# Gathers of 128 rows instead of 96 in a mixture-of-experts layer, and an index copy moved from VectorE to ScalarE

## The chip, the core and the metric

The kernel runs on one core of a Trainium2 chip. The core has five engines that run side by side: TensorE (PE; its weight loads are shown apart as PEld), VectorE (DVE), ScalarE (ACT), GpSimd (POOL) and SyncE (SP). They meet only through semaphores. Data moves between HBM and on-chip memory (SBUF) through 16 DMA engines, which the queues of SP and of POOL share. The metric is the device time of one execution in microseconds (us); less is better. Before the change it is 1160.18 us, the median of 3 runs (1159.56 to 1162.26).

## The reference

One decoder layer for 512 tokens of width 1024: two attention branches, and then a mixture of experts (MoE). Only the second part matters here:

```python
scores = jax.nn.sigmoid(h @ w_router)                      # 64 experts
_, top_idx = lax.top_k(scores + router_bias, 8)            # 8 experts for a token
top_w = take(scores, top_idx) / sum(...) * 2.5
...
hg = xb @ w_gate_e[e];  hu = xb @ w_up_e[e]                # 1024 -> 256, for each expert
hmid = silu(hg) * hu * gate
routed += hmid @ w_down_e[e]                               # 256 -> 1024
...
x = x1 + routed + swiglu(h, w_gate_s, w_up_s, w_down_s)    # a shared expert for all tokens
```

512 tokens with 8 experts each are 4096 pairs of token and expert, 64 to an expert in the mean. All weights and activations are float32.

## The kernel before

The first part of the program computes attention and the routing. The second, from about 500 us on, is a pipeline over 68 items: 4 tiles of tokens through the shared expert (`SH = 4`), then 64 experts. The change lies in the pipeline of the experts.

An expert has `SLOTS = 96` slots. A matmul against a one-hot matrix (`find_slots`) finds the token of each slot, and `read_idx` (line 1258, VectorE) writes the token indices to `idxg`, one to a partition. A slot without a token gets an index of 1024 or more (`NO_TOKEN`), which lies above the bounds check (511), and the DMA skips its row. Which slot stands on which partition is set by a table made on the host, line 1822, with `DMA_ENGINES = 16`:

```python
c[:, P:P + SLOTS] = np.arange(SLOTS).reshape(SLOTS // DMA_ENGINES, DMA_ENGINES).T.reshape(-1)[None]
```

Partitions 0 to 5 so hold slots 0, 16, 32, 48, 64 and 80, partitions 6 to 11 slots 1, 17, 33 and so on.

For expert k the work goes through the engines as follows.

- **SP** loads the expert's three weights (1 MB each) into one of four slots (`load_w`, line 470). A load waits until the expert four places earlier has been split.
- **POOL** gathers the expert's token rows (4 KB each) from `hn_dram` into `xg` (line 566), up to five experts ahead, and later adds the expert's output rows to `out` in HBM (the scatter, line 572). The loop `pair` issues scatter k and then gather k + 5. A scatter waits until the one before has landed. Ahead of each transfer stands a tiny operation, `turn` (line 562), that keeps their order.
- **ScalarE** (`step`) rounds weights to their high parts (`gu_hi_k`, line 863; `split_wd`, line 814), applies SiLU, copies the turned tokens, and writes the output rows to one of two buffers `y` (line 831), for which the scatter of two experts earlier must have landed.
- **VectorE** (`expert`) subtracts to get the low parts of the weights (lines 1290 and 1300), multiplies by the gate, and makes the indices and one-hot matrices of later experts.
- **PE** multiplies with three products of high and low parts for each matmul (lines 1669 and 1683), turns the gathered rows (line 1697), and finds slots.

Each engine's program is a fixed list in this order; a semaphore wait holds back all that stands behind it. `idxg` is overwritten for expert k + 4 before the scatter of k may have been issued, so a second copy, `idxs`, is made for the scatter (line 1397, VectorE), and the semaphore `idx_kept` counts these copies.

Of the kernel before, what the change touches and what calls it, by code (L numbers as in the profile page):

```python
# [41 lines left out]
SLOTS = 96  # L42
DMA_ENGINES = 16
WARM_UP = 56
NO_TOKEN = 1024
# [4 lines left out]
def layer(nc, x, g_mix, w_in, q_norm_a, k_norm_a, q_norm_b, k_norm_b, rel_bias, b_forget, w_gate, b_gate,  # L50
# [98 lines left out]
    with ctx:  # L149
# [25 lines left out]
        idxg = [sb(f"idxg{i}", [P, 1], u32) for i in range(4)]  # L175
# [150 lines left out]
        def after(eng, s, n):  # L326

            if not isinstance(n, int) or n > 0:
                eng.wait_ge(s, n)  # L329
# [199 lines left out]
        def _(pool):  # L529
            nc.gpsimd.memset(minus_half[:], -0.5).then_inc(pool_set, 1)  # L530
            pool.wait_ge(pool_set, 1)

            def root(dst, src, n, width):

# [18 lines left out]
                pool.wait_ge(tr_ready[b], uses[b])  # L553
            for i in range(4):
                nc.gpsimd.memset(xg[i], 0.0).then_inc(pool_set, 1)
            pool.wait_ge(pool_set, 5)
            last_row = pool.to_reg(N - 1)

            def take_turn(before):
# [3 lines left out]

            def gather(slot, before, done):
                take_turn(before)
                pool.indirect_dma_start(out=xg[slot][0:SLOTS, :], out_offset=None, in_=hn_dram,  # L566
                                        in_offset=bass.IndirectOffsetOnAxis(idxg[slot][0:SLOTS, 0:1], 0),
                                        bounds_check=last_row, oob_is_err=False).then_inc(done, 16)

            def scatter(slot, idx, before, done):  # L570
# [48 lines left out]
        def _(act):  # L619
# [246 lines left out]
            def xT_hi_k(k):  # L866
# [4 lines left out]
                for c in range(2):  # L871
                    nc.scalar.activation(xT_hi[:, c * HALF:(c + 1) * HALF, :], turned_rows(c), ACT.Copy).then_inc(xT_hi_ready, 1)

            def step(it, n, slot, more=True):
                k = it - SH
                if more:
                    for c in range(CHUNKS - 1):
                        gu_hi_k(k + 1, (slot + 1) % 4, c)
# [17 lines left out]
            for it in range(SH):  # L896
# [9 lines left out]
                if it == SH - 2:  # L906

                    act.wait_ge(hn_ready, NT)
                    act.wait_ge(onehot_ready, 1)
                    act.wait_ge(logits_psum, 1)  # L910
                    for c in range(CHUNKS - 1):
                        gu_hi_k(0, 0, c)
            for c in range(CHUNKS - 1):
                gu_hi_k(1, 1, c)
            silu_i(SH, 0, SLOTS)
# [32 lines left out]
        def _(dve):  # L948
# [432 lines left out]
            def expert(k, u, ix=True, oh=True, xt=True):  # L1381
# [11 lines left out]
                    low_wd(u, 0, last_hi, last_lo).then_inc(wd_ready, 1)  # L1393
                if isinstance(k, int) and k == 0:
                    y_shared(SH - 1)
                after(dve, scattered, 16 * (k - 3))
                nc.vector.tensor_copy(idxs[u][0:SLOTS, :], idxg[u][0:SLOTS, :]).then_inc(idx_kept, 1)
                low_midT_i(SH + k, u % 2, SLOTS)
                if ix:
                    dve.wait_ge(mid_ready, SH + k + 1)  # L1400
# [457 lines left out]
```

## Time and profile before

| | |
|---|---|
| median of 3 runs | 1160.18 us (1159.56 to 1162.26) |
| profiled execution, device time | 1161.51 us |
| its span in the profile | 1159.5 us |
| PE busy | 1112.1 us (96%) |
| DVE busy | 875.7 us (76%) |
| ACT busy | 719.9 us (62%) |
| POOL busy | 363.3 us (31%) |
| DMA | 284.64 MB, mean 245 GB/s, 65606 packets |
| clock granted to PE, mean | 0.986 of full |

The profile is of one execution. Its span runs from the first to the last instruction; the device time has 2.0 us more around it. An engine's busy share is a mean over the whole program, and stages differ, so the rows below are mostly of stretches. "L863" is line 863 of the kernel; the releaser behind an arrow is what ended the idle time. The DMA share is the mean over 16 engines of the time that their packets took; packets overlap a little, so it can exceed 1. PE's busy time is modelled and PE at 100% need not be at its peak.

### The profile page before, as it was taken

What the parts mean: (1) busy time and instruction counts of PE and PEld (TensorE: products, weight loads), DVE (VectorE), ACT (ScalarE), POOL (GpSimd) and SP (SyncE); (2) the same over time, 40 slices, a digit from 0 to 9 for tenths busy, and PEclk for the clock granted to TensorE, in tenths of its full rate; (3) what the DMA queues carried; (4) which work ended last, traced back from release to release, by engine and by line L of the source; (5) the groups of instructions that cost most, each with busy time, mean ns of one, the idle gap of its engine ahead of it and who ended that gap; (6) DMA issues with size and microseconds to landing.
All of it is one profiled execution on the core that took longest, in us unless ns stands there. A gap on an engine that the chain in (4) does not pass through costs nothing.

```text
span 1159.5 us, 18735 instructions
## 1 busy us (share of the span) xinstructions
PE 1112.1 (96%) x5682; PEld 826.2 (71%) x5682; DVE 875.7 (76%) x1445; ACT 719.9 (62%) x1218; POOL 363.3 (31%) x293
## 2 busy tenths in 40 slices
PE   7999999999999999999999999999999999989994
PEld 5889978777775575567777777777676767766762
DVE  6443476578753534589999999989898989989982
ACT  5434455453435121268888888878787878877882
POOL 0221021000000001136333344344345344568842
PEclk7999999999999999999999999999999999999998
DMA  5333221412422275459999999999999999999952
GB/s 188 123 96 119 78 74 37 155 65 78 123 85 80 67 324 209 159 216 384 368 365 365 370 372 367 367 364 371 366 367 367 355 359 365 371 361 357 365 184 34
DMA packets 65606, 284.64 MB, mean 245 GB/s; under 512 B 12515, under 2 KB 15083, under 8 KB 40604
## 3 DMA queue, kind: packets, MB, share of 16 engines
q1 hardware_dynamic: 51228, 250.50, 57.5%
q0 software_dynamic: 14336, 33.59, 12.2%
q8 instruction: 25, 0.41, 0.1%
q14 instruction: 17, 0.14, 0.0%
HBM read 271.40 MB, written 29.42 MB: 259 GB/s over the span
## 4 chain that ended last, share of the span: by engine, by line
DMA 47%; POOL 4%; issue 3%; POOLq 1%; ACT 0%; DVE 0%
DMA out<-arena,idxs 47%; POOL turn L562 4%; POOLq L329 0%; POOL out L572 0%; POOLq L578 0%; ACT arena L831 0%; POOL arena L566 0%; POOLq L598 0%; POOLq L582 0%; DVE w_lo L1295 0%; POOLq L583 0%
## 5 line engine op out<-in xcount | busy, mean ns | idle before, releaser
L1669 PE MATMUL bank<-gu_parts,xT_parts 128*96 128x512 f32 x1280 | 343.8, 398 | 3.1 <-DVE xT_parts L1283 2.5
L562 POOL TENSOR_TENSOR turn<-minus_half 16x1 f32<-16x1 f32 x128 | 174.1, 1360 | 341.9 <-DMA out<-arena,idxs 289.2
L1669 PEld LDWEIGHTS bank<-gu_parts,xT_parts 128*96 128x96 f32 x1280 | 202.5, 162 | 86.2 <-DVE xT_parts L1283 2.9
L1683 PE MATMUL bank<-w_lo 128*96 128x512 f32 (+1 forms) x804 | 200.3, 397 | 0.9 <-DVE w_lo L1295 0.9
L1683 PEld LDWEIGHTS bank<-w_lo 128*96 128x96 f32 (+1 forms) x804 | 128.0, 166 | 46.7 <-DVE w_lo L1295 1.1
L1500 PE MATMUL bank<-w_hi,hT_hi 128*128 128x512 f32 (+1 forms) x320 | 125.8, 393 | 3.1 <-DVE arena L1241 1.7
L1290 DVE TENSOR_TENSOR gu_parts<-arena_x,gu_parts 128x1024 fp32r<-128x1024 f32 x96 | 116.7, 1215 | 12.5 <-ACT gu_parts L863 12.5
L1290 DVE TENSOR_TENSOR gu_parts<-arena,gu_parts 128x1024 fp32r<-128x1024 f32 x96 | 116.6, 1215 | 11.3 <-ACT gu_parts L863 11.3
L1500 PE MATMUL bank<-w_hi,hT_lo 128*128 128x512 f32 (+1 forms) x320 | 122.7, 383 | 0.0
L1500 PE MATMUL bank<-w_lo,hT_hi 128*128 128x512 f32 (+1 forms) x320 | 122.4, 383 | 0.0
L863 ACT ACTIVATE gu_parts<-arena_x 128x1024 fp32r<-128x1024 f32 x96 | 101.4, 1056 | 27.6 <-DMA arena_x<-in_w_up_e 18.8
L863 ACT ACTIVATE gu_parts<-arena 128x1024 fp32r<-128x1024 f32 x96 | 101.4, 1056 | 24.0 <-DMA arena<-in_w_up_e 20.1
L572 POOL DMA_INDIRECT out<-arena,idxs x64 | 107.3, 1676 | 16.2 <-issue 14.2
L991 DVE TENSOR_TENSOR w_lo<-arena,w_hi 128x512 fp32r<-128x512 f32 (+1 forms) x112 | 69.1, 667 | 47.9 <-ACT w_hi L648 47.9
L831 ACT ACTIVATE arena<-bank 96x512 f32<-96x512 f32 x128 | 73.2, 591 | 31.5 <-PE bank L1683 19.9
L1669 PE MATMUL bank<-gu_more,xT_parts 128*96 128x512 f32 x256 | 90.8, 395 | 0.0
L536 POOL TENSOR_TENSOR hn_r<-hn_ms,minus_half 128x1 f32<-128x1 f32 x8 | 4.4, 555 | 254.7 <-DVE hn_ms L961 254.7
L536 POOL TENSOR_TENSOR rnorm<-mean,minus_half 128x8 f32<-128x8 f32 x20 | 32.7, 1637 | 156.5 <-DVE mean L1054 156.5
L648 ACT ACTIVATE w_hi<-arena 128x512 fp32r<-128x512 f32 (+1 forms) x112 | 61.4, 605 | 32.1 <-PE bank L1500 20.5
L1697 PEld LDWEIGHTS bank<-cst,arena 96*128 96x128 f32 x512 | 66.5, 203 | 15.2 <-DMA arena<-hn_dram,idxg 7.1
L1300 DVE TENSOR_TENSOR w_lo<-arena_x,w_lo 128x1024 fp32r<-128x1024 f32 x64 | 75.2, 1214 | 1.2 <-ACT w_lo L814 1.2
L1300 DVE TENSOR_TENSOR w_lo<-arena,w_lo 128x1024 fp32r<-128x1024 f32 x64 | 75.2, 1214 | 0.9 <-ACT w_lo L814 0.9
(194 smaller groups left out, 1934.9 us busy)
## 6 DMA issues: line engine op xcount, KB each, us to landing
arena<-in_w_gate_e SPq DMA_DIRECT2D x32, 1024.0 KB
arena<-in_w_up_e SPq DMA_DIRECT2D x32, 1024.0 KB
arena<-in_w_down_e SPq DMA_DIRECT2D x32, 1024.0 KB
arena_x<-in_w_gate_e SPq DMA_DIRECT2D x32, 1024.0 KB
arena_x<-in_w_up_e SPq DMA_DIRECT2D x32, 1024.0 KB
arena_x<-in_w_down_e SPq DMA_DIRECT2D x32, 1024.0 KB
arena<-in_w_in SPq DMA_DIRECT2D x14, 1024.0 KB, 5.4
arena<-in_w_gate SPq DMA_DIRECT2D x8, 1024.0 KB, 5.8
```

What stands on the lines that cost most here:

```text
L562: nc.gpsimd.tensor_tensor(turn[:], minus_half[0:16, 0:1], minus_half[0:16, 0:1], ALU.add).then_inc(turns, 1)
L572: pool.indirect_dma_start(out=out_rows, out_offset=bass.IndirectOffsetOnAxis(idx[0:SLOTS, 0:1], 0), in_=y[slot][0:SLOTS, :], in_offset=Non ...
L648: nc.scalar.activation(split_of(w_hi, c, j), raw_of(c, j), ACT.Copy).then_inc(split_hi, 1)
L831: return nc.scalar.activation(y[n][0:SLOTS, h * 512:(h + 1) * 512], psY[h][0:SLOTS, :], ACT.Copy)
L863: nc.scalar.activation(gu_hi[c].rearrange("p g j c -> p g (j c)"), wgu[slot][:, :, PER * c:PER * (c + 1), :].rearrange("p g j c -> p g (j ...
L991: nc.vector.tensor_tensor(split_of(w_lo, c, j), raw_of(c, j), split_of(w_hi, c, j).bitcast(f32), ALU.subtract).then_inc(split_lo, 1)
L1290: nc.vector.tensor_tensor(flat(gu_lo[c]), flat(raw_part), flat(gu_hi[c]).bitcast(f32), ALU.subtract).then_inc(gu_lo_ready, 1)
L1300: return nc.vector.tensor_tensor(low[:, :, cols], wd[slot][:, :, cols], high[:, :, cols].bitcast(f32), ALU.subtract)
L1500: last = nc.tensor.matmul(psD[n % 2][:, 0:chunk_cols(c)], left, right, start=(j == 0 and k == 0), stop=(j == ND - 1 and k == 2))
L1669: last = nc.tensor.matmul(out_, a[:, PER * c + j, :], b[c][:, :, j, :], start=(c == 0 and j == 0 and i == 0), stop=(c == CHUNKS - 1 and j ...
L1683: last = nc.tensor.matmul(psY[h][0:rows, :], midT[n][a][:, j, 0:rows], w[b][:, j, h * 512:(h + 1) * 512], start=(j == 0 and k == 0), stop= ...
L1697: last = nc.tensor.transpose(psT[j // HALF][:, c:c + SLOTS], xg[slot][0:SLOTS, j::ND], ident[0:SLOTS, 0:SLOTS])
```

## The change

A gather now has 128 rows. Its index list is the whole of `idxg`, whose last 32 entries are set once, at the start, to `NO_TOKEN` and never again, so the last 32 rows are always skipped. The slot table of line 1822, the scatter (96 rows) and the number of transfers stay. The copy of `idxg` to `idxs` goes from VectorE, where it stood behind the expert's last gate and up split, to ScalarE, at the head of each `step`. The diff:

```diff
@@ POOL @@
             nc.gpsimd.memset(minus_half[:], -0.5).then_inc(pool_set, 1)
             pool.wait_ge(pool_set, 1)
+            for i in range(4):
+                nc.gpsimd.memset(idxg[i][SLOTS:, :], NO_TOKEN).then_inc(pool_set, 1)
+                pool.wait_ge(pool_set, i + 2)
...
-            pool.wait_ge(pool_set, 5)
+            pool.wait_ge(pool_set, 9)
...
             def gather(slot, before, done):
                 take_turn(before)
-                pool.indirect_dma_start(out=xg[slot][0:SLOTS, :], out_offset=None, in_=hn_dram,
-                                        in_offset=bass.IndirectOffsetOnAxis(idxg[slot][0:SLOTS, 0:1], 0),
+                pool.indirect_dma_start(out=xg[slot], out_offset=None, in_=hn_dram,
+                                        in_offset=bass.IndirectOffsetOnAxis(idxg[slot][:, 0:1], 0),
                                         bounds_check=last_row, oob_is_err=False).then_inc(done, 16)
@@ ScalarE @@
+            def keep_idx(k, u):
+                act.wait_ge(idx_ready, k + 1)
+                after(act, scattered, 16 * (k - 3))
+                nc.scalar.activation(idxs[u][0:SLOTS, :], idxg[u][0:SLOTS, :], ACT.Copy).then_inc(idx_kept, 1)
+
             def step(it, n, slot, more=True):
                 k = it - SH
+                keep_idx(k, slot)
                 if more:
...
+            keep_idx(0, 0)
             for c in range(CHUNKS - 1):
                 gu_hi_k(1, 1, c)
@@ VectorE @@
-                after(dve, scattered, 16 * (k - 3))
-                nc.vector.tensor_copy(idxs[u][0:SLOTS, :], idxg[u][0:SLOTS, :]).then_inc(idx_kept, 1)
                 low_midT_i(SH + k, u % 2, SLOTS)
```

POOL's list in the loop over experts, before and after. A row is an instruction with its line, what it writes and reads, its shape, and the semaphores it waits for:

```order
L566 DMA arena<-hn_dram,idxg 96x1024
L582 REGISTER_ALU
L329 REGISTER_ALU [waits idx_kept,y_ready]
L329 ISA [waits scattered]
L562 TENSOR_TENSOR turn<-minus_half 16x1 [waits turns]
L572 DMA out<-arena,idxs 512x1024
```

```order
L569 DMA arena<-hn_dram,idxg 128x1024
L585 REGISTER_ALU
L329 REGISTER_ALU [waits idx_kept,y_ready]
L329 ISA [waits scattered]
L565 TENSOR_TENSOR turn<-minus_half 16x1 [waits turns]
L575 DMA out<-arena,idxs 512x1024
```

Only the gather's rows have changed, 96 to 128; order and waits are the same (512x1024 is the whole of `out`; the scatter's index list still has 96 entries).

ScalarE's list around the end of one step and the start of the next, in the loop, before and after:

```order
L814 ACTIVATE w_lo<-arena 128x2x512 [waits y_psum] x2
L924 REGISTER_ALU
L924 COMPARE_AND_BRANCH
L863 ACTIVATE gu_parts<-arena_x 128x1024 [waits gu_part,w_slot1_u,w_slot1_g]
L863 ACTIVATE gu_more<-arena_x 128x1024 [waits gu_part,w_slot1_u,w_slot1_g]
```

```order
L817 ACTIVATE w_lo<-arena 128x2x512 [waits y_psum] x2
L934 REGISTER_ALU
L934 COMPARE_AND_BRANCH
L880 ACTIVATE idxs<-idxg 96x1 [waits scattered,idx_ready]
L866 ACTIVATE gu_parts<-arena_x 128x1024 [waits gu_part,w_slot1_u,w_slot1_g]
L866 ACTIVATE gu_more<-arena_x 128x1024 [waits gu_part,w_slot1_u,w_slot1_g]
```

The index copy, with its two waits, stands ahead of the first weight split of each step. On VectorE it is gone, and nothing else has moved there.

## Rows read from the trace of the kernel before

**Rows 1.** The page's 40 slices: PE and DMA in tenths busy, GB/s.

```profile
PE   7999999999999999999999999999999999989994
...
DMA  5333221412422275459999999999999999999952
GB/s 188 123 96 119 78 74 37 155 65 78 123 85 80 67 324 209 159 216 384 368 365 365 370 372 367 367 364 371 366 367 367 355 359 365 371 361 357 365 184 34
```

**Rows 2.** Busy time by stretch; then PEclk, DMA share, GB/s.

```profile
core 0: us, PE busy (x) PEld busy (x) DVE busy (x) ACT busy (x) POOL busy (x), PEclk, DMA share, GB/s
450.00:500.00 50.00, 46.25 (x173) 24.79 (x172) 26.67 (x75) 9.90 (x17) 7.87 (x10) 1.00 0.57 220
525.00:575.00 50.00, 50.00 (x263) 37.40 (x263) 49.16 (x73) 42.81 (x63) 24.79 (x18) 1.00 1.02 378
575.00:775.00 200.00, 199.50 (x1034) 148.12 (x1033) 193.18 (x292) 171.04 (x248) 81.95 (x84) 1.00 1.03 367
775.00:1000.00 225.00, 219.17 (x1098) 160.32 (x1097) 204.25 (x308) 178.50 (x264) 99.68 (x87) 0.99 1.02 365
1000.00:1120.00 120.00, 112.77 (x571) 81.87 (x570) 107.30 (x155) 93.92 (x138) 86.91 (x46) 1.00 0.98 346
1120.00:1160.00 40.00, 23.21 (x108) 16.40 (x106) 17.45 (x25) 17.48 (x27) 12.04 (x10) 0.86 0.25 36
```

**Rows 3.** Waits from 550 to 775 us, total, times, longest.

```profile
ACT gu_parts L863 <- DMA arena<-in_w_up_e: 2.9, 2, 1.8
```

**Rows 4.** Waits from 775 to 1120 us.

```profile
ACT gu_parts L863 <- DMA arena_x<-in_w_up_e: 18.6, 10, 3.3
ACT gu_parts L863 <- DMA arena<-in_w_up_e: 17.3, 8, 3.3
ACT arena L831 <- DMA out<-arena,idxs: 11.1, 10, 4.5
```

**Rows 5.** POOL in order of time (start, duration), 680 to 694 us.

```profile
681.79 1.45 POOL L572 DMA_INDIRECT out<-arena,idxs  x1 [0.16 <-issue]
...
690.02 1.23 POOL L562 TENSOR_TENSOR turn<-minus_half 16x1 f32<-16x1 f32 x1 [4.78 <-DMA out<-arena,idxs]
691.40 1.45 POOL L572 DMA_INDIRECT out<-arena,idxs  x1 [0.16 <-issue]
```

**Rows 6.** Two scatters on POOL, from 790 us.

```profile
790.42 1.45 POOL L572 DMA_INDIRECT out<-arena,idxs  x1 [0.16 <-issue]
...
800.33 1.45 POOL L572 DMA_INDIRECT out<-arena,idxs  x1 [0.16 <-issue]
```

**Rows 7.** The page's DMA queues: packets, bytes, share of 16 engines.

```profile
q1 hardware_dynamic: 51228, 250.50, 57.5%
q0 software_dynamic: 14336, 33.59, 12.2%
```

**Rows 8.** Issues of expert weights: ns min/median/max, first and last start.

```profile
L470 SPq DMA_DIRECT2D arena<-in_w_down_e x32: 328/333/515, 408.0 to 1105.5; - x32
```

**Rows 9.** The page's chain that ended last.

```profile
DMA 47%; POOL 4%; issue 3%; POOLq 1%; ACT 0%; DVE 0%
```

**Rows 10.** Line 572, the scatter, issue to landing.

```profile
DMA to landing us min/median/max: 4.6/8.8/11.6
```

**Rows 11.** POOL in order of time, 1038 to 1062 us.

```profile
1038.88 1.00 POOL L566 DMA_INDIRECT arena<-hn_dram,idxg  x1 [0.15 <-issue]
...
1041.35 1.45 POOL L572 DMA_INDIRECT out<-arena,idxs  x1 [0.16 <-issue]
...
1051.51 1.45 POOL L572 DMA_INDIRECT out<-arena,idxs  x1 [0.16 <-issue]
```

**Rows 12.** Line 1397, VectorE's index copy, ns min/median/max.

```profile
L1397 DVE COPY idxs<-idxg x64: 138/143/147, 511.5 to 1139.8; 96x1 uint32<-96x1 uint32 x64
```

**Rows 13.** ScalarE's smallest copy, by form.

```profile
L721 ACT ACTIVATE frow<-bank 128x8 f32<-128x8 f32 x4 | 0.7, 171 | 4.4 <-PE bank L1500 4.4
```

## The prediction, made before the changed kernel was run

> **What bounds the kernel now.** I read the slices of the page first. From slice 19 on (about 525 us) PE reads 9 and the DMA line is also 9, at 355 to 384 GB/s [rows 1]. So two resources look full at once, and only a view by stage can part them. The windows do: from 525 to 1000 us the 16 DMA engines show a share of 1.02 to 1.03 (packets overlap, so a full engine reads a little over 1), from 1000 to 1120 us 0.98, and 0.25 after the last weights [rows 2]. Before, at 450 to 500 us, it was 0.57. PE is busy at full clock for 199.5 of 200 us up to 775 us, and then loses 5.8 of 225 us and 7.2 of 120 us [rows 2].
>
> Third come the waits. Up to 775 us ScalarE waits for expert weights (line 863, the first to touch them) for only 2.9 us in all, after that for 18.6 + 17.3 = 35.9 us [rows 3, 4]. That is a prefetch running out: four weight slots give a lead, PE takes an expert every 9.6 us (scatters issued at 681.79 and 691.40) [rows 5], the DMA engines take longer, and at about 775 us the lead is gone. From there an expert takes some 10 us [rows 6].
>
> What the DMA engines need can be worked out from the queues [rows 7]. The weight queue was busy 57.5% of 16 engines: 0.575 x 16 x 1159.5 = 10,667 us for 250.50 MB, or 42.6 us per MB. An expert's 3.146 MB are then 134 us, 8.4 us on each engine. The gather and scatter queue took 12.2%, 2,263 us; over 64 experts that is 35.4 us, 2.2 us on each engine. Together 10.6 us, or 10.4 at a share of 1.02: the pace seen after 775 us, and above PE's 9.6. Since the average engine has no idle time from 525 us to the last weights, the fullest has none either, and a load has landed only when all of its engines are done. The end is therefore that of the fullest DMA engine, plus a tail that doesn't change: the last w_down load is issued at 1105.5 us [rows 8], the engines are empty soon after 1120 us, and the span ends at 1159.5.
>
> The chain of waits names something else, the scatters: 47% of the span, one after the other [rows 9]. A scatter lands 8.8 us after its issue [rows 10], and the next waits for it. But what the scatters hold up is only the buffer y, and line 831 waits for that 11.1 us in all, 10 times after 775 us, against 35.9 us for weights [rows 4]. I take this chain as a second bound lying just beneath the first.
>
> **The change, part by part.** The gather. Queue 0 had 14,336 packets [rows 7]: 128 transfers of 96 rows and 16 completions are 128 x 112 = 14,336, so a skipped row is still a packet, a tiny one. Its 33.59 MB are 8,192 rows of 4,096 B, 64 x 64 gathered and as many scattered. With 32 more rows to a gather there are 64 x 32 = 2,048 more empty packets and not a byte more.
>
> What changes is who does the work. The kernel's own slot table (line 1822) puts slot s into row 6 x (s mod 16) + s div 16: six rows in a row for each of 16 DMA engines, with consecutive slots on different engines. This deals any number of tokens evenly, provided that an engine gets six consecutive rows. With 128 rows an engine gets eight, and the table is not changed. Dealt eight in a row, the 96 live rows fall on engines 0 to 11, and engines 12 to 15 gather nothing.
>
> The rows can be counted, since routing the reference's own inputs tells each expert's tokens (44 to 91, 4,096 in all). In the kernel before, the fullest engine gathers 286 rows and scatters 286, the emptiest 226 and 226. After, with eight in a row, the fullest gathers 414. The first five gathers go out ahead of all scatters, while the engines still have idle time (share 0.57 at 450 to 500 us) [rows 2]; without them it is 266 rows before and 384 after, 118 more.
>
> The Trainium skill has another deal for 128 partitions ("DMA: Bandwidth & Descriptors", the descriptor swizzle): engine 0 takes rows 0 to 3 and 32 to 35, and so on, so that engines 8 to 15 have four live rows each and engines 0 to 7 eight. By it the fullest engine gathers 376 rows from expert 5 on, 110 more, and scatters 4 fewer: 110 x 0.174 - 4 x 0.378 = 17.6 us. Nothing in this trace shows a 128-row gather; either deal has engines with eight live rows, and that is what counts.
>
> The price of a gathered row, 4,096 B: at the weight queue's 42.6 us per MB it is 0.174 us. The mean of queue 0 is 2,263 / 8,192 = 0.276 us [rows 7], over gathers and scatters. A scatter adds to what is in HBM and has to read as well, so the gather is the cheaper of the two: 0.174 is the lower end, 0.276 the upper, and I take 0.174, as a plain transfer (a scattered row is then 2 x 0.276 - 0.174 = 0.378). Sum: 118 x 0.174 = 20.5 us. As the deal isn't shown, and one with fewer live rows on the fullest engine would give less, I take 19 us. The bounds are 0 (an even deal) and 118 x 0.276 = 32.6 us.
>
> Nothing hides this: the fullest engine has no idle time, and the prefetch lead is spent already; it would only be spent sooner. Before, that engine lay 30 rows above the mean of 256 both ways, 30 x 0.552 = 16.6 us; the change more than doubles this.
>
> POOL issues a gather in 1.00 us [rows 11]; 128 rows instead of 96 may cost up to 1.33 us. Behind it stands only the next scatter, and POOL is idle 4.78 us before it, for a landing [rows 5], so nothing is lost. After 1000 us that cover is gone at times (gather at 1038.88, the next scatter 2.47 us later) [rows 11]: at most 0.33 x 12 = 4 us, if scatters set the pace there. With weights coming later still they don't, and I add nothing. The four memsets of index tails stand at the program's start, ahead of POOL's first wait for VectorE: nothing. A row of SP isn't moved, and no transfer is added.
>
> The index copy. DVE loses 64 copies of 143 ns [rows 12], 9.2 us. ScalarE gains 64; the nearest row is a 128x8 copy of 171 ns [rows 13], 10.9 us in all. Its waits stop nothing: the indices were needed by the gather long before, and the count of scatters that it wants (16(k-3)) is the one that the previous step's y copy already waited for. Behind it on ScalarE stands the first weight split of line 863, which itself waits for weights when these are late; in the stage where PE sets the pace ScalarE is busy 171 of 200 us [rows 2]. If that cover failed it would cost up to 10.9 us. DVE is busy 193 of 200 us there, and could give back up to 9.2 us if it set the pace, but a faster compute stage only runs down the lead sooner. Both zero.
>
> Sum: profiled run 1161.5 us (span 1159.5 and 2.0 around it) + 19 = 1180.5; against the median of 1160.2, 1.3 us lower, 1179. I say 1180.
>
> **The rivals.** *An even deal.* The rows of a gather could go round the engines one by one, or the index list could be split by live rows. Then only 2,048 tiny packets are added: 1160 us, within 0.2%. Against it: the slot table makes sense only for consecutive rows. Chance 11%.
>
> *Scatters set the pace.* After 1000 us the share is 0.98, and the scatters follow 10.16 us apart (1041.35 and 1051.51) [rows 11]. If their chain bounds that stage, weights have slack there, and the cost is what a gather directly ahead delays a scatter: 1.33 to 2 more live rows on an engine, each with a weight packet of 8 KB in between, (0.174 + 0.349) x 1.33 to 2 = 0.7 to 1.0 us, for some 12 to 17 experts: 8 to 17 us, middle 11, so 1171 us. Chance 12%.
>
> *Wide gathers are faster.* This one ends on the other side. If a gathered row costs the mean of 0.276 us now because an engine's six rows don't suit the way it writes them, and 0.174 once they are dealt by eight, the fullest engine goes from 266 x 0.276 = 73.4 us to 384 x 0.174 = 66.8, or 376 x 0.174 = 65.4: 7 to 8 us less, 1153 us. It decides when more than 0.085 us of a row's time goes away (266 x 0.276 = 384 x 0.191). The trace has no row for a gathered packet alone; the mean holds the dear scatters, which makes this unlikely. The Trainium skill speaks for it ("SBUF — State Buffer", section "Can I just issue two DMAs to hit both halves?"): the only way to reach all 16 ports is one transfer over all 128 partitions. No row here shows ports. Chance 7%.
>
> *The upper price.* A row costs 0.276 us or more, in queueing with weight packets: 1191 us and above. Chance 5%.
>
> **How the numbers follow.** The forecast, fuller engines at 0.15 to 0.24 us a row (110 x 0.15 = 16.5 to 118 x 0.24 = 28, so 1176 to 1189), holds 65%. A range that leaves out no more than 2 in 10 has to take in the scatters' case and the upper half of the even deal: 1160 to 1190 us. What a measurement here can tell from no change is about 0.2%, 2.3 us. Faster: 7% for wide gathers and 2% from the even deal, 0.09. Same: the rest of that, 0.09. Slower: 0.82.
>
> **What would show it.** Right: queue 0 with 16,384 packets at the same 284.64 MB; in the windows GB/s from 575 to 1120 us down by about 3%, and a mean share below 1 while weights are waited for, which an even deal can't give; line 863's waits for weights above the 2.9 + 35.9 = 38.8 us of now [rows 3, 4], starting well before 775 us; an expert every 10.3 to 10.6 us instead of some 10. Scatters as the pace: line 831's waits for DMA grow beyond those for weights. Wrong: the same GB/s and share as before, or a stage between 575 and 775 us as fast as now followed by one no slower. DVE's 64 copies gone and ScalarE's 64 near 0.17 us would show the copy; if ScalarE had idle time before them on scatters, my zero there is wrong.

## The result, and the profile after

The changed kernel takes 1151.05 us in the median of 20 runs (1140.92 to 1172.72), the kernel before 1160.12 us beside it (20 runs, 1157.49 to 1173.89): ratio 0.9891, 95% interval 0.9863 to 0.992. The forecast was 1180 us, range 1160 to 1190, with 0.09 for faster. It was wrong in sign. The ratios leave out every execution that took over 1.5% longer than the fastest of its kernel: 6 of the 20 here, 14 of 31 of wide_only and its two repeats below, and 1 of 71 of the kernel before, so a median over all runs shows less gain than a ratio. The profile below is of a second set of runs of the changed kernel (after_again, 1149.74 us, 1143.07 to 1152.68, 6 runs; ratio 0.9849, 0.9797 to 0.9901). Its span is 1150.5 us against 1159.5.

The page of the changed kernel, its slices, queues and chain:

```profile
span 1150.5 us, 18761 instructions
...
PE   7999999999999999999999999999999999898995
...
DMA  5333221422422184459999999999999999998962
GB/s 183 131 97 116 83 68 44 148 73 75 128 74 92 41 335 193 184 199 395 380 378 377 378 378 376 378 382 380 380 377 378 378 376 373 332 343 288 368 207 32
...
q1 hardware_dynamic: 51228, 250.50, 56.6%
q0 software_dynamic: 16384, 33.60, 11.8%
...
DMA 41%; PE 38%; DVE 7%; POOL 5%; issue 5%; ACT 2%; POOLq 1%; SPq 0%; ACTq 0%; DVEq 0%
```

Queue 0 has the 2,048 packets more that were counted, and 33.60 MB instead of 33.59. But more packets took less time. The share of q0 is 11.8% of a span of 1150.5, that is 0.118 x 16 x 1150.5 = 2,172 us, where before it was 2,263 [rows 7]. And q1, which the change doesn't touch, took 0.566 x 16 x 1150.5 = 10,419 us for the same 250.50 MB, where before it was 10,667. Each load of weights moves faster, though nothing was done to it: this is the first sign of the cause. PE, which was not in the chain of [rows 9], now has 38% of it.

The windows of the changed kernel, to be laid beside [rows 2]:

```profile
525.00:575.00 50.00, 50.00 (x263) 37.37 (x262) 48.85 (x69) 43.16 (x69) 29.52 (x20) 1.00 1.02 383
575.00:775.00 200.00, 200.00 (x1040) 148.72 (x1039) 192.81 (x272) 173.50 (x270) 75.62 (x83) 1.00 1.02 378
775.00:1000.00 225.00, 222.56 (x1149) 164.84 (x1148) 209.49 (x297) 187.20 (x295) 102.85 (x91) 1.00 1.01 375
1000.00:1120.00 120.00, 110.87 (x535) 80.24 (x536) 102.99 (x138) 93.43 (x147) 70.44 (x46) 0.96 0.87 304
```

The share stays at 1.02 and 1.01 up to 1000 us, so the engines are as full as they were there, but what they move rises from 367 to 378 GB/s and from 365 to 375. PE, which lost 5.8 of 225 us between 775 and 1000 us, loses 2.4. The waits for weights and for the buffer y, for [rows 3, 4]; line 863 is 866 now, and line 831 is 834. From 550 to 775 us no wait of line 866 is left. From 775 to 1120 us:

```profile
ACT arena L834 <- DMA out<-arena,idxs: 17.4, 7, 6.4
...
ACT gu_parts L866 <- DMA arena_x<-in_w_up_e: 5.8, 4, 2.6
ACT gu_parts L866 <- DMA arena<-in_w_up_e: 5.0, 6, 1.2
```

Weights are waited for 10.8 us where it was 38.8, and y for 17.4 where it was 11.1. The second bound, the scatters, lay just beneath the first, as the prediction said, and came out when the first went down. Of 28 us of waits for weights that go, the span keeps 9.

Even of these 9 us only a part belongs to the pipeline. The last scatter lands at 1152.5 us before and at 1147.5 after, 5.0 us earlier. Behind it stands GpSimd's closing instruction, DRAIN, for which all engines wait, and it takes 4.4 us less. Before, then after:

```profile
L149 POOLq DRAIN  x1: 6558/6558/6558, 1152.7 to 1152.7; - x1
```

```profile
L149 POOLq DRAIN  x1: 2194/2194/2194, 1147.7 to 1147.7; - x1
```

It is 6.558 us in all three profiled versions of the layer with gathers of 96 rows (before, copy_only, narrow_plain) and 2.194 us in all seven profiles with gathers of 128. So it comes with the wide gather, but what sets it is open: no experiment was made on it, and stream and deal, which have both widths each, show 6.920 and 1.852.

The rows for [rows 12] and [rows 10], ScalarE's index copy, and the landings of the scatter (line 575), with those of the gather (line 569) behind them:

```profile
L880 ACT ACTIVATE idxs<-idxg x64: 190/193/213, 498.1 to 1128.1; 96x1 uint32<-96x1 uint32 x64
```

```profile
DMA to landing us min/median/max: 4.4/8.6/15.1
...
DMA to landing us min/median/max: 3.6/9.6/11.3
```

### The profile page after: what moved, and what is told of

Read it like the earlier page. It is cut to its first block, busy times and chain, and to the rows that moved or that the text cites. A ratio compares the mean times of both kernels' runs of the same rounds, so it can differ in the third digit from the quotient of the medians.

```text
span 1164.9 us, 18761 instructions
## 1 busy us (share of the span) xinstructions
PE 1109.7 (95%) x5682; PEld 820.0 (70%) x5682; DVE 876.3 (75%) x1381; ACT 730.0 (63%) x1282; POOL 569.0 (49%) x297
## 3 DMA queue, kind: packets, MB, share of 16 engines
q1 hardware_dynamic: 51228, 250.50, 56.4%
q0 software_dynamic: 16384, 33.60, 12.4%
## 4 chain that ended last, share of the span: by engine, by line
PE 42%; DMA 28%; POOL 13%; DVE 7%; issue 6%; ACT 3%; POOLq 0%; SPq 0%; ACTq 0%; DVEq 0%
PE bank L1508 19%; DMA out<-arena,idxs 18%; POOL turn L565 12%; DMA arena<-hn_dram,idxg 9%; PE bank L1691 5%; PE bank L1677 4%; PE bank L1457 2%; PE bank L1665 2%; PE bank L1651 2%; PE bank L1705 1%; DVE w_lo L1001 1%; PE bank L1647 1%; DVE gu_parts L1300 1%; ACT arena L739 1%; DMA arena<-in_w_out 1%
## 5 line engine op out<-in xcount | busy, mean ns | idle before, releaser
L565 POOL TENSOR_TENSOR turn<-minus_half 16x1 f32<-16x1 f32 x128 | 357.2, 2791 | 142.4 <-DMA out<-arena,idxs 81.1
L575 POOL DMA_INDIRECT out<-arena,idxs x64 | 113.8, 1778 | 20.2 <-issue 18.0
L1705 PEld LDWEIGHTS bank<-cst,arena 96*128 96x128 f32 x512 | 64.1, 203 | 44.6 <-DMA arena<-hn_dram,idxg 25.2
L875 ACT ACTIVATE xT_parts<-bank 128x384 fp32r<-128x384 f32 x128 | 56.0, 489 | 63.1 <-PE bank L1705 63.1
L1705 PE MATMUL bank<-cst,arena 96*128 96x96 f32 x512 | 69.1, 278 | 24.6 <-DMA arena<-hn_dram,idxg 24.1
L569 POOL DMA_INDIRECT arena<-hn_dram,idxg x64 | 84.6, 1322 | 10.3 <-issue 2.3
```

The source lines that it names most:

```text
L565: nc.gpsimd.tensor_tensor(turn[:], minus_half[0:16, 0:1], minus_half[0:16, 0:1], ALU.add).then_inc(turns, 1)
L569: pool.indirect_dma_start(out=xg[slot], out_offset=None, in_=hn_dram, in_offset=bass.IndirectOffsetOnAxis(idxg[slot][:, 0:1], 0), bounds_c ...
L575: pool.indirect_dma_start(out=out_rows, out_offset=bass.IndirectOffsetOnAxis(idx[0:SLOTS, 0:1], 0), in_=y[slot][0:SLOTS, :], in_offset=Non ...
L1705: last = nc.tensor.transpose(psT[j // HALF][:, c:c + SLOTS], xg[slot][0:SLOTS, j::ND], ident[0:SLOTS, 0:SLOTS])
```

## The experiments

**Which half of the change does it?** wide_only is the kernel before with the wide gather, and VectorE still copies the indices:

```diff
-pool.wait_ge(pool_set, 5)
+for i in range(4):
+    nc.gpsimd.memset(idxg[i][SLOTS:, :], NO_TOKEN).then_inc(pool_set, 1)
+...
+pool.wait_ge(pool_set, 9)
-pool.indirect_dma_start(out=xg[slot][0:SLOTS, :], ... idxg[slot][0:SLOTS, 0:1] ...)
+pool.indirect_dma_start(out=xg[slot], ... idxg[slot][:, 0:1] ...)
```

> Only the gather's part of the change: 128 rows, index tails set once; VectorE still copies the indices. Theory 1 (the 128-row gather takes load off the DMA engines: each gathered row becomes cheaper and no longer stretches weight packets): the whole gain, ratio about 0.989, some 1148 us. Theory 2 (the gain comes from taking the 0.14 us copy off VectorE, which is nearly full): no gain, 1160 us. The prediction's own mechanism (fullest engine with eight live rows) would give 1180 us, and is all but excluded by the changed kernel's 1151.

copy_only is the other half: 96 rows, and ScalarE copies.

```diff
+def keep_idx(k, u):   # ScalarE
+    act.wait_ge(idx_ready, k + 1)
+    after(act, scattered, 16 * (k - 3))
+    nc.scalar.activation(idxs[u][0:SLOTS, :], idxg[u][0:SLOTS, :], ACT.Copy).then_inc(idx_kept, 1)
-after(dve, scattered, 16 * (k - 3))
-nc.vector.tensor_copy(idxs[u][0:SLOTS, :], idxg[u][0:SLOTS, :]).then_inc(idx_kept, 1)
```

> Only the copy's part of the change: ScalarE copies the indices, gathers have 96 rows as before. Theory 1: no change, 1160 us within 2 us. Theory 2: the whole gain, some 1150 us.

after_again is the changed kernel beside both, on the same chip.

> The changed kernel once more, on the same chip as its two halves: ratio about 0.989 to the kernel before. Theory 1 expects the weight splits on ScalarE not to wait for weights, GB/s no lower than before, and a time within 3 us of the gather's part alone. Theory 2 expects it to be as fast as the copy's part alone.

Measured, against 1165.06 us of the kernel before on that chip: wide_only 1142.62 us (1139.51 to 1174.39, 7 runs), ratio 0.9793 (0.9738 to 0.9848); copy_only 1162.25 (1156.27 to 1171.6, 12 runs), ratio 1.0004 (0.9964 to 1.0043); after_again 0.9849. The gather has all of the gain, the copy none that can be measured. After_again and wide_only overlap in their intervals, so a small price of ScalarE's copy isn't excluded, and none is shown. The windows of copy_only are those of before:

```profile
575.00:775.00 200.00, 199.50 (x1035) 148.23 (x1034) 191.21 (x270) 170.94 (x268) 80.60 (x83) 1.00 1.03 367
775.00:1000.00 225.00, 220.04 (x1102) 160.50 (x1101) 204.34 (x287) 180.23 (x288) 92.74 (x88) 1.00 1.02 367
```

**How are the rows dealt, and what does one cost?** deal computes nothing of the layer: it runs 22 indirect transfers one at a time, with chosen live rows and all others skipped. In short:

```diff
+"run6": [0, 1, 2, 3, 4, 5], "run8": [0 .. 7], "step6": [0, 6, 12 .. 90], "step16": [0, 16 .. 80],
+"four_and_four": [0, 1, 2, 3, 32, 33, 34, 35], "slots64": the places of 64 tokens by the slot table
+for each of gather 96, gather 128, scatter 96: issue, wait for its landing, next
```

> No part of the layer: gathers of 96 and of 128 rows and adding scatters of 96 rows, one at a time, each waited for, with only chosen rows live (4 KB each). Of one transfer the time from issue to landing and the number of data packets that run side by side tell which rows share an engine. Deal by consecutive rows: 6 live rows in a run land one after the other in a 96-row gather (about 6 x 0.16 us) and 8 in a run in a 128-row one. Deal by four and four: a run of 8 in a 128-row gather is split over two engines (4 x 0.16 us), and rows 0 to 3 with 32 to 35 share one (8 x 0.16 us). Deal round the engines one by one: rows 0, 16, 32 ... share one, and a run of 8 lands in one packet's time. With 64 rows live in the kernel's slot order the fullest engine has 4 rows at 96; 6 to 8 by either deal at 128. The prediction needs the last.

Measured (100.02 us in all) from the packets of each transfer: the time from the first live row's start to the last one's end, and how many were under way at once.

```
gather of 96, rows 0 to 5              6 rows   1252 ns   at most 2 at once
gather of 96, rows 0, 6, 12 .. 90     16 rows    538 ns            15
gather of 128, rows 0 to 7             8 rows    969 ns             3
gather of 128, rows 0 to 5             6 rows    682 ns             2
gather of 128, rows 0-3 and 32-35      8 rows   1732 ns             2
scatter of 96, rows 0 to 5             6 rows   2434 ns             2
scatter of 96, rows 0, 6, 12 .. 90    16 rows    749 ns            16
```

GpSimd's own rows show the same: what stands in brackets is the wait for the transfer issued one row above. First the gathers of 96 with six rows in a row and with every sixth, then those of 128 with four and four, and with all 96.

```profile
12.51 1.15 POOL L62 DMA_INDIRECT xg<-in_x,idxu  x1 [10.82 <-issue]
16.20 0.99 POOL L62 DMA_INDIRECT xg<-in_x,idxu  x1 [2.55 <-DMA xg<-in_x,idxu]
19.05 0.96 POOL L62 DMA_INDIRECT xg<-in_x,idxu  x1 [1.86 <-DMA xg<-in_x,idxu]
...
52.19 0.99 POOL L62 DMA_INDIRECT xg<-in_x,idxu  x1 [2.08 <-DMA xg<-in_x,idxu]
56.20 0.99 POOL L62 DMA_INDIRECT xg<-in_x,idxu  x1 [3.02 <-DMA xg<-in_x,idxu]
60.21 0.99 POOL L62 DMA_INDIRECT xg<-in_x,idxu  x1 [3.02 <-DMA xg<-in_x,idxu]
```

At 96 an engine has six rows in a row. At 128 the eight rows 0 to 7 go to two engines, and rows 0 to 3 with 32 to 35 are all on one: four and four. The Trainium skill has the same deal for 128 partitions ("DMA: Bandwidth & Descriptors", the descriptor swizzle). The fullest engine gathers 376 rows from expert 5 on, not 384. Alone, a gathered row takes 159 ns in the median in both widths and a scattered one 328; with 0.174 and 0.378 us the prediction was 9% and 15% too high. Issuing takes GpSimd 0.96 to 0.99 us at 96 (the very first 1.15), 0.99 to 1.01 at 128. So the deal was as feared, and the prices nearly so. Something else moved.

**Does the fullest engine set the end?** narrow_plain is the kernel before with slot s in row s, so the first tokens of each expert share engines:

```diff
-np.arange(SLOTS).reshape(SLOTS // DMA_ENGINES, DMA_ENGINES).T.reshape(-1)[None]
+np.arange(SLOTS)[None]
```

> The kernel before, with 96-row gathers and scatters, but slot s on partition s. Engines still take six rows in a run (shown by the lone transfers), so engines 0 to 6 now gather and scatter 384 rows each instead of 286 at most, and the last ones nearly none. Theory 1 (the fullest DMA engine sets the end, as the prediction had it): 98 rows more, at 0.16 to 0.19 us for a gathered and 0.32 us for a scattered row, 47 to 50 us, so some 1208 us. Rival (the engines share one limit, and only their mean counts): 1160 us, no change.

Measured 1210.8 us (1209.98 to 1213.87, 4 runs) against 1160.05: ratio 1.0435 (1.0389 to 1.048). The fullest engine scatters 98 rows more, and gathers 98 more, or 88 from expert 5 on. At 0.33 and 0.19 us (as rows measure in this kernel, below) these are 49 us, and 50.8 came. The weight packets also grew here, by 8 ns in the mean (335.9 to 343.7 ns from 525 to 1125 us), which would add 11 us and isn't in that sum. So it is shown that an uneven deal costs about what its fullest engine has more, within some 10 us. The share drops below 1, as engines that are less full idle:

```profile
575.00:775.00 200.00, 187.88 (x947) 134.84 (x947) 175.86 (x265) 151.25 (x224) 152.82 (x78) 1.00 0.97 339
775.00:1000.00 225.00, 210.35 (x1014) 151.31 (x1013) 188.08 (x281) 162.76 (x243) 83.17 (x84) 0.97 0.95 333
```

even_slots goes the other way: wide_only with a slot table that is balanced for both deals, six in a row for the scatter and four and four for the gather.

```diff
-np.arange(SLOTS).reshape(SLOTS // DMA_ENGINES, DMA_ENGINES).T.reshape(-1)[None]
+np.array(SLOT_OF)[None]     # SLOT_OF = [89, 43, 27, 83, 32, 61, 80, 1, ...]
```

> 128-row gathers, VectorE copies, and a slot table that deals live rows evenly for a gather dealt four and four and a scatter dealt by six. By rows alone the fullest engine has 128 us of gather and scatter work instead of 158 (0.16 and 0.33 us a row). Theory 1a (both: foreign partitions make rows dearer at 96, and the fullest engine still sets the pace late in the 128-row version): weights no longer arrive late anywhere, an expert every 9.6 us to the end, 1138 to 1141 us, with the landings of one load's 16 engines within 3 us of each other. Theory 1b (with 128 rows the uneven deal doesn't matter): the same as the gather's part alone, 1142 us, and landings spread as there.

Measured 1141.4 us (1140.33 to 1146.85, 5 runs), ratio 0.984 (0.9801 to 0.9879).

```profile
575.00:775.00 200.00, 200.00 (x1041) 148.76 (x1041) 194.25 (x294) 173.47 (x250) 72.38 (x84) 1.00 1.02 382
775.00:1000.00 225.00, 223.16 (x1153) 165.55 (x1152) 215.24 (x323) 191.97 (x278) 93.30 (x92) 0.99 1.01 377
```

The 16 parts of one expert's last load land apart by how uneven the engines' work was up to then. Their spread, in us:

```
expert           5      20     34     44
before          2.6     9.1   18.7   20.6
after_again     2.3     7.1   13.5   18.4
even_slots      1.7     1.6    1.8    2.2
narrow_plain    5.7    16.8   22.4   21.2
```

So the unevenness is real, in the changed kernel too, and the table takes it out. Yet it is worth little. In even_slots ScalarE waits from 550 to 1120 us neither for weights nor for y, and the last packet of weights lands at 1094.9 us, where it is 1108.6 in after_again and 1111.7 in wide_again, the profile of the wide gather alone (below). But the spans of even_slots and wide_again are 1138.9 and 1140.7 us. With wide gathers the fullest engine hardly sets the end any more; what is left is PE.

**What makes every packet faster?** stream computes nothing of the layer either: 20 loads of 1 MB run back to back in each of nine phases, and in seven of them 12 indirect transfers of 64 live rows go one after the other, of which some 7 fall beside the loads.

```diff
+PHASES = [("none", 0), ("gather", 96), ("gather", 128), ("none", 0), ("scatter", 96), ("scatter", 128),
+          ("gather", 128, live rows moved up by 32), ("gather", 96), ("gather", 128)]
```

> No part of the layer: 1 MB weight loads back to back from SyncE (20 in each phase, four in flight) beside 12 indirect transfers with 64 live rows, in nine phases: none; gathers of 96; of 128; none; scatters of 96; of 128; gathers of 128 with the live rows on partitions 32 to 127; gathers of 96; of 128. Theory 1a: a weight packet (8 KB) takes 309 ns in the median in all phases, but beside 96-row gathers a fair part take 400 ns and more, and gathered rows (4 KB) 180 ns and more in the mean; beside 128-row gathers both stay near 309 and 159. The phase of 128-row gathers with live rows on 32 to 127 is as clean. Rival (it was only the phase of the two streams in the real kernel): the same packet times at 96 and 128.

Measured (702.6 us in all), in the order of the phases: the phase, how long its loads took, the mean of a weight packet of 8 KB, the share of them above 380 ns, and the mean of a live row that starts while the loads run.

```
none          50.64 us   314.8 ns   0.005     -
gather 96     59.85      339.1      0.163   204.7 ns
gather 128    57.80      317.8      0.024   165.3
none          51.10      315.7      0.005     -
scatter 96    59.73      318.5      0.022   328.3
scatter 128   61.99      321.3      0.030   348.0
gather 128^   57.39      316.3      0.022   167.8     (^ live rows 32 to 127)
gather 96     59.08      334.8      0.141   192.9
gather 128    58.14      317.9      0.025   165.1
```

This is the effect, by itself. Beside a gather of 96 rows one weight packet in six or seven is stretched from 0.31 to over 0.38 us, and the gather's own rows take 193 to 205 ns in the mean. Beside a gather of 128 rows with the same 64 live ones it is one weight packet in forty, and the rows take 165 to 168. A scatter of 96, which reads SBUF and writes HBM, stretches few weight packets either, and with 128 rows they are no shorter (321.3 against 318.5 ns). The same in the layer, 800 to 900 us (mean and 90th percentile of a weight packet, mean of a gathered and median of a scattered row, ns; gathered and scattered packets are told apart by their durations, below and above 300):

```
before          336   418   195   327
copy_only       334   404   189   327
after_again     323   324   159   327
even_slots      322   324   160   327
```

Over all of 525 to 1125 us the means are 335.9 ns before and 327.3 in after_again for a weight packet, and 192.1 and 159.7 for a gathered row.

The likely reason is where an engine writes. By the Trainium skill ("DMA: Bandwidth & Descriptors", The descriptor swizzle) each engine of a 128-partition transfer writes the partitions of one SBUF port and no other. With six rows in a row that can't hold, so at 96 an engine would write through ports at which the weight loads keep other engines busy. The port is argued, as no row shows one, and no run varied it by itself; the stretching, its near end at 128 rows and the two deals are shown.

**Wide gather again, and the even table beside it.**

> The gather's part alone once more, beside the version with evenly dealt slots: 1142 us, ratio 0.98 to 0.985. In an undisturbed execution the fullest engine's lag behind the emptiest grows over the experts (theory 1a).

Measured 1151.14 us (1140.3 to 1172.51, 12 runs), ratio 0.987 (0.9835 to 0.9904), so the median over all runs came 9 us above the 1142 expected, and the ratio just outside the range. Its profile (span 1140.7) shows 379 and 374 GB/s:

```profile
575.00:775.00 200.00, 200.00 (x1043) 148.98 (x1042) 194.25 (x293) 173.16 (x251) 71.76 (x84) 1.00 1.02 379
775.00:1000.00 225.00, 223.34 (x1151) 165.41 (x1150) 213.77 (x322) 187.53 (x275) 99.33 (x91) 1.00 1.01 374
```

even_again is even_slots, and wide_third wide_only, side by side on another chip.

> The slot table balanced for the deal of four and four, beside the same kernel with the old table (wide_third) on the same chip. If the uneven deal (fullest engine 406 gathered rows, mean 256) still costs time once the gathers are wide, this one is 2 to 6 us faster in the median, 1140 against 1144, and its range narrower. If with wide gathers PE sets the pace for nearly the whole expert stage, the two medians lie within 2 us.

> The gather of 128 rows alone, copy on VectorE, old slot table: 1141 to 1150 us, ratio to the kernel before 0.98 to 0.99. The wider part of that range means that the chain of scatters falls behind in some executions; the balanced table should not show it if the fullest engine is what starts it.

Measured: even_again 1148.15 us (1141.38 to 1150.9, 6 runs), ratio 0.9884 (0.985 to 0.9918); wide_third 1162.44 (1141.91 to 1167.5, 12 runs), with a ratio of 0.9906 (0.9863 to 0.9948). Both medians miss what was expected (1140 us for even_again, 1141 to 1150 for wide_third), and wide_third's, over all its runs, lies above the 1159.89 of the kernel before beside it. The intervals of the ratios overlap, as those of the first pair do (0.984 and 0.987). Whether the even table is worth more than the wide gather alone isn't settled; what stands is that none of its 11 runs passed 1150.9 us, where 14 of the 31 with the wide gather alone passed 1159. It beats the kernel before in both sets, and has the lowest ratio of its set each time; that it beats the changed kernel isn't shown.

**Who holds GpSimd?** The profile of even_again is 7 us longer than that of even_slots, and one difference stands out: for a while GpSimd's turn, an addition of 16x1 before each gather and scatter, takes 6 us instead of 1. held tries VectorE as the cause. It computes nothing of the layer. In short:

```diff
+for i in range(6):                       # VectorE, back to back, by phase
+    nc.vector.tensor_tensor(lo[i], a, hi, ALU.subtract)       # both in SBUF; or one in a bank; or a copy
+pool.wait_ge(runs, n + 1)                # GpSimd: after the first of the six
+nc.gpsimd.tensor_tensor(turn, minus_half, minus_half, ALU.add)
```

> No part of the layer: VectorE runs operations on 128x1024 back to back, six to a run, and GpSimd is told to do its 16x1 addition (the turn of the gathers and scatters) when the first of the six is done. Five phases of four runs: one VectorE operation alone, then nothing; six with both operands in SBUF; six of 128x512 with one operand in a PSUM bank; six copies; six with both operands in SBUF again. If VectorE's operations with two SBUF operands hold GpSimd off, the turn takes 1.1 us in the first phase and, in the second and fifth, as long as the five operations that are left, 5 x 1.21 = 6.1 us; with one operand in a bank it takes 1.1 us. If the 5.6 to 6.6 us seen in the layer come from something else (DMA, GpSimd's own descriptors), the turn takes about 1.1 us in all five.

GpSimd's rows, one for each phase in turn: VectorE does nothing more; two operands in SBUF; one in a bank; copy; two in SBUF again.

```profile
8.54 0.18 POOL L72 TENSOR_TENSOR turn<-minus_half 16x1 f32<-16x1 f32 x1 [1.40 <-DVE lo L56]
...
20.34 1.03 POOL L72 TENSOR_TENSOR turn<-minus_half 16x1 f32<-16x1 f32 x1 [6.00 <-DVE lo L56]
...
44.71 0.18 POOL L72 TENSOR_TENSOR turn<-minus_half 16x1 f32<-16x1 f32 x1 [3.63 <-DVE lo L58]
...
59.99 0.50 POOL L72 TENSOR_TENSOR turn<-minus_half 16x1 f32<-16x1 f32 x1 [3.33 <-DVE lo L60]
...
79.06 1.04 POOL L72 TENSOR_TENSOR turn<-minus_half 16x1 f32<-16x1 f32 x1 [6.00 <-DVE lo L56]
```

The turn takes 0.18 us by itself, so the 1.1 us expected for the first phase was itself such a hold. Two SBUF operands on VectorE hold it for 1.03 us, which is to the end of the operation under way (1.22 us each), and not for the four that follow: the expectation of 6.1 us failed. Half of it is shown, that VectorE's kind of operation decides; why a hold spans five operations in the layer stays open.

## Why the prediction was wrong

*The bound* was right for the kernel before. Its DMA engines read full at a share of 1.02 to 1.03, and moving rows onto the fullest engine cost 50.8 us in narrow_plain for 49 worked out. It did not stay the bound: the changed kernel's share is 0.87 from 1000 to 1120 us, and an even deal of the wide gather's rows gains little.

*The deal* was right in what counts. The fullest engine gathers 110 rows more from expert 5 on (four and four), and the spread of landings shows it still uneven.

*The price of a row* was nearly right: 0.159 us against 0.174 taken, and 0.328 against 0.378 for a scattered one. The 110 rows cost 110 x 0.159 = 17.5 us, less 4 x 0.328 = 1.3: 16.2, where the forecast had 19.

*The step that failed* is one that the prediction never wrote down as a term: that the packets which were there already keep their durations. "With 32 more rows to a gather there are 64 x 32 = 2,048 more empty packets and not a byte more" was followed by "What changes is who does the work", and by nothing on how long the work of everyone else takes. On the fullest engine, from expert 5 on (59 experts, 24 weight packets each), with the means of 525 to 1125 us:

```
more rows                  +110 x 0.159 - 4 x 0.328           +16.2 us
gathered rows, unstretched  266 x (0.1921 - 0.1597)            -8.6
weight packets              59 x 24 x (0.3359 - 0.3273)       -12.2
sum                                                            -4.6
```

The sum has the sign, and the larger term is in the weight queue, on which the change has no line. It doesn't have the size. The last packet of weights lands 15.1 us earlier in after_again (1123.7 to 1108.6 us) and 12.0 earlier in wide_again, whose weight packets are at 325.2 ns, for a sum of -7.6. The means are over all engines, and no row tells which engine a packet is on, so what the fullest one gained beyond them stays open.

A second step failed, "a tail that doesn't change". From the last packet of weights to the end of the span it is 35.8 us before, 41.9 in after_again and 29.0 in wide_again. GpSimd's DRAIN gives back 4.4 us in both. The rest goes with the scatters: in after_again the scatter of expert 44 is issued 12.8 us earlier than before (952.8 against 965.6), the last one only 4.7 earlier (1143.1 against 1147.8).

The mean of queue 0, 0.276 us, could not show the stretching, but the weight queue could. Its packets of 8 KB took 336 ns in the mean, where the same packet took 315 in stream with nothing beside it. That a part of the packets was stretched stood in the trace, in the distribution of their durations (median 318 ns, 90th percentile 418), and the prediction took the mean of the queue for the price of a plain transfer.

*The rival "wide gathers are faster"* had nearly the right end (1153 us) for partly the right reason, at 7%. That its number came so close is partly luck: it put the gain into the gathered row alone and asked 0.085 us of it, and the row gave 0.032. The weight packets and the DRAIN gave more. The sentence of the Trainium skill beside it ("SBUF — State Buffer", "Can I just issue two DMAs to hit both halves?", one transfer over all 128 partitions reaches all 16 ports) pointed the right way. stream agrees as far as times go: 339 and 335 ns for a weight packet beside 96 rows, 318 beside 128. No row shows ports.

*What goes late next.* The forecast had weights land later; they land sooner, so the prefetch lead lasts longer. ScalarE's waits for weights begin at 877 us and not 765, when the scatters are at expert 36 and not 24, and PE sets the pace of 9.6 us until then. The last part of the w_down loads of experts 24 to 44 lands every (935.8 - 727.0) / 20 = 10.44 us before and (921.4 - 719.1) / 20 = 10.12 after. Then the scatters' chain takes over earlier. Past 1000 us line 834 waits for it 10.4 us, where line 831 waited 10.8; between 775 and 1000 us it is 17.4 - 10.4 = 7.0 us, where it was 11.1 - 10.8 = 0.3. From 1000 us on, before and then after:

```profile
ACT arena L831 <- DMA out<-arena,idxs: 10.8, 9, 4.5
```

```profile
ACT arena L834 <- DMA out<-arena,idxs: 10.4, 4, 6.4
```

That is the second bound of the prediction, and with PE it is what is left in this profile. In those of even_slots and even_again it isn't there either (0.0 and 0.4 us), which leaves PE and fits the even table adding little.

*The other rivals.* The deal was not even, the scatters took no 11 us from the sum, and a row didn't cost 0.276 us: each fell to a row of deal or to the ratio itself.

*GpSimd and the copies* were right at zero. The issue takes 0.04 us longer at 128 rows (1.04 us against 1.00 in the layer), and copy_only stands at 1.0004. ScalarE's copy is 193 ns against 171 taken.

Of what the prediction said would show it right, the 16,384 packets came, and the rest didn't: GB/s rose by 3% from 575 to 1000 us and did not fall, line 866 waits for 10.8 us and not above 38.8, and no share below 1 came before 1000 us. Of its list for "wrong" the last came, a stage between 575 and 775 us as fast as now followed by one no slower. The list also named the same GB/s as before; that they might rise was in no part of the text.

## What to carry to other kernels

Where transfers share DMA engines, a change to one has two prices: how many packets the fullest engine gets, and how long every other packet on the engines then takes. Look at the distribution of packet times, not at the mean of a queue: a large minority of long ones (here 418 ns at the 90th percentile, and 319 in stream's first phase) says that two transfers disturb each other, and that a shape which doesn't may pay for more rows. For an indirect gather into SBUF beside full-width loads, 128 rows with the last ones skipped were cheaper than 96; for a scatter out of SBUF they weren't. And read the end of the program before a gain is put down to a stage: here 4.4 of the 9 us came behind the last transfer.

## What the hardware showed beyond that

- Skipped rows cost about nothing to issue or move: 2,048 more of them, 14 us more for queue 0's packets of 4 B in the layer, under 1 us on each engine, and 0.99 to 1.01 us for an issue at 128 rows against 0.96 to 0.99 at 96.
- An indirect transfer of 96 rows is dealt six in a row to each engine (rows 0 to 5 one after the other, 1252 ns), one of 128 four and four (rows 0 to 3 with 32 to 35, 1732 ns).
- VectorE's operations with both operands in SBUF hold GpSimd off. The Trainium skill has this as an exclusive lock on a pair of ports that the two share ("SBUF — State Buffer", "Who interferes with whom"), and held agrees: 0.18 us free or beside an operand from a bank, 1.03 us beside two SBUF operands, 0.50 beside copies. In the layer the hold can be longer. GpSimd of even_again, the turn after a scatter's issue, and then VectorE's run (lines 1304 and 1294 have both operands in SBUF):

```profile
688.03 1.90 POOL L576 DMA_INDIRECT out<-arena,idxs  x1 [0.53 <-issue]
689.45 6.55 POOL L566 TENSOR_TENSOR turn<-minus_half 16x1 f32<-16x1 f32 x1
696.15 1.04 POOL L570 DMA_INDIRECT arena<-hn_dram,idxg  x1
```

```profile
690.19 2.35 DVE L1304 TENSOR_TENSOR w_lo<-arena_x,w_lo 128x1024 fp32r<-128x1024 f32 x2
692.46 1.21 DVE L1294 TENSOR_TENSOR gu_parts<-arena,gu_parts 128x1024 fp32r<-128x1024 f32 x1
693.60 1.22 DVE L1294 TENSOR_TENSOR gu_parts<-arena,gu_more 128x1024 fp32r<-128x1024 f32 x1
694.74 1.21 DVE L1294 TENSOR_TENSOR gu_parts<-arena,gu_parts 128x1024 fp32r<-128x1024 f32 x1
695.87 0.47 DVE L1271 SCALAR_TENSOR_TENSOR arena_x<-arena_x,gate,bank 96x256 f32<-96x256 f32 x1
```

The turn ends at 696.00 us, as VectorE's five end (695.95), and the gather goes out 6 us late. From 550 to 775 us GpSimd is busy 158.41 us in this profile and PE 219.44 of 225; in that of even_slots it is 81.43 and 225.00:

```profile
550.00:775.00 225.00, 219.44 (x1129) 160.84 (x1128) 213.38 (x318) 188.79 (x271) 158.41 (x90) 1.00 1.01 370
```

```profile
550.00:775.00 225.00, 225.00 (x1168) 167.31 (x1167) 218.51 (x329) 195.51 (x281) 81.43 (x93) 1.00 1.02 383
```

The two executions of one kernel differ by 7 us of span (1146.1 and 1138.9); as far as the traces show, by whether the turn meets the start of VectorE's run, which no experiment separated. The hold is in other profiles too. From 520 us on, GpSimd has 10 turns or issues of over 3 us before and 11 in after_again, but 24 in even_again, and 52 and 53 in two long executions that were profiled, the changed kernel at a span of 1164.9 us and wide_only at 1172.5. In these two GpSimd is busy 174 and 178 of 200 us and PE loses 9.6 and 8.7, while ScalarE waits for no weights from 550 to 1120 us:

```profile
575.00:775.00 200.00, 190.40 (x978) 138.35 (x976) 182.76 (x253) 161.82 (x254) 174.13 (x80) 1.00 0.99 357
```

```profile
575.00:775.00 200.00, 191.34 (x975) 138.37 (x974) 184.18 (x273) 162.05 (x234) 177.71 (x79) 1.00 1.00 359
```

So the hold goes with the longer executions, and whether it makes them long isn't shown. A kernel with another operation in the turn's place wasn't tried.
